# The middle tap of the last FFN's convolution made on ScalarE, with the weight cast of each half's last tile behind it

## The reference

```python
h = rms_norm_2(x, g_ffn[l])
up = depthwise_conv(h @ w_up[l], conv_f_w[l], conv_f_b[l], FFN_CONV // 2)
act = jax.nn.gelu(up[..., :D_FF_2], approximate=True) * up[..., D_FF_2:]
x = x + act @ w_down[l]
```

## Time and profile before

| what | us |
|---|---|
| median of three runs | 1883.85 |
| the profiled execution, its time | 1883.64 |
| the profiled execution, its span | 1881.9 |
| TensorE busy (matmuls) | 1855.5 |
| VectorE busy | 1243.5 |
| ScalarE busy | 523.6 |
| up phases of the last FFN, start of their first unit to end of their last | 1489 to 1626, 1695 to 1807 |

### The profile page before, as it was taken

One profiled execution on the slowest core, in us unless ns is written; L12 is line 12 of the kernel. 1 busy time (PEld: TensorE's weight loads), 2 busy tenths in 40 slices (PEclk: granted clock), 3 DMA queues, 4 the chain that ended last, 5 costly groups with the idle time before them and its releaser, 6 DMA issues.

```text
span 1881.9 us, 21566 instructions
## 1 busy us (share of the span) xinstructions
PE 1855.5 (99%) x8620; PEld 1482.7 (79%) x8620; DVE 1243.5 (66%) x1670; ACT 523.6 (28%) x481; POOL 15.4 (1%) x57
## 2 busy tenths in 40 slices
PE   8999999999999999999999999999999999999997
PEld 6888888878888778888888888877778888788875
DVE  6763667667745487443244779979975788726874
ACT  5333222122322222221122112148852122212210
POOL 0000000000000000000000000000000000000000
PEclk9999999999999999999999999999999999999998
DMA  5224341472111332222322224232224222232221
GB/s 203 89 82 153 111 157 64 149 263 99 68 68 46 112 134 76 103 84 84 122 90 72 84 90 157 90 112 85 76 70 162 90 90 98 75 104 103 81 72 71
DMA packets 48132, 194.64 MB, mean 103 GB/s; under 512 B 6720, under 2 KB 15296, under 8 KB 33344
## 3 DMA queue, kind: packets, MB, share of 16 engines
q1 hardware_dynamic: 48064, 193.70, 29.9%
HBM read 180.84 MB, written 12.85 MB: 103 GB/s over the span
## 4 chain that ended last, share of the span: by engine, by line
PE 77%; issue 20%; DVE 3%; DMA 0%; ACT 0%; POOLq 0%; POOL 0%; SPq 0%; DVEq 0%
PE bank L942 23%; PE bank L943 23%; PE bank L944 23%; PE xb L1217 2%; DVE wlo L1292 1%; PE xb L1163 0%; PE xb L1153 0%; PE bank L1059 0%; PE bank L1060 0%; PE bank L1061 0%; PE xb L1171 0%; PE xb L981 0%; PE xb L1120 0%; PE xb L974 0%; DVE x L1336 0%
## 5 line engine op out<-in xcount | busy, mean ns | idle before, releaser
L942 PE MATMUL bank<-uhi,whi 128*128 128x512 f32 x1552 | 622.9, 401 | 7.2 <-DVE wlo L2138 7.0
L943 PE MATMUL bank<-ulo,whi 128*128 128x512 f32 x1552 | 616.7, 397 | 0.0
L944 PE MATMUL bank<-uhi,wlo 128*128 128x512 f32 x1552 | 616.6, 397 | 0.0
L654 ACT ACTIVATE whi<-raw 128x2048 fp32r<-128x2048 f32 (+3 forms) x177 | 299.9, 1694 | 1101.8 <-PE bank L944 1073.1
L1292 DVE TENSOR_TENSOR wlo<-raw,whi 128x2048 fp32r<-128x2048 f32 (+3 forms) x177 | 356.5, 2014 | 80.3 <-ACT whi L654 77.9
L942 PEld LDWEIGHTS bank<-uhi,whi 128*128 128x128 f32 x1552 | 293.3, 189 | 80.2 <-issue 9.7
L944 PEld LDWEIGHTS bank<-uhi,wlo 128*128 128x128 f32 x1552 | 293.3, 189 | 71.6
L943 PEld LDWEIGHTS bank<-ulo,whi 128*128 128x128 f32 x1552 | 293.6, 189 | 71.0 <-issue 1.4
L942 PE MATMUL bank<-hhi,whi 128*128 128x512 f32 x528 | 209.8, 397 | 2.3 <-DVE hlo L1345 1.2
L943 PE MATMUL bank<-hlo,whi 128*128 128x512 f32 x528 | 209.3, 396 | 0.0
L944 PE MATMUL bank<-hhi,wlo 128*128 128x512 f32 x528 | 209.3, 396 | 0.0
(11 more groups left out here) (391 smaller groups left out, 1815.4 us busy)
## 6 DMA issues: line engine op xcount, KB each, us to landing
raw<-in_up SPq DMA_DIRECT2D x65, 1024.0 KB, 4.8
raw<-in_win SPq DMA_DIRECT2D x16, 1024.0 KB, 4.8
raw<-in_wout SPq DMA_DIRECT2D x8, 1024.0 KB, 4.9
raw<-in_down1a SPq DMA_DIRECT2D x8, 768.0 KB, 4.4
tab<-tab_kept SPq DMA_DIRECT2D x4, 1536.0 KB, 8.6
raw<-in_down2a SPq DMA_DIRECT2D x8, 768.0 KB, 4.4
raw<-in_down3a SPq DMA_DIRECT2D x8, 768.0 KB, 4.3
raw<-in_down1b SPq DMA_DIRECT2D x8, 640.0 KB, 4.0
```

Source lines behind the costliest of these rows:

```text
L654: act.activation(whi[s][:, 0:width], raw[s][:, 0:width], ACT.Copy).then_inc(w_hi, 1)
L942: pe.matmul(dst, wh, hi, start=first, stop=False)
L943: pe.matmul(dst, wh, lo, start=False, stop=False)
L944: return pe.matmul(dst, wl, hi, start=False, stop=last)
```

## The change

ScalarE makes the middle tap and the bias of both halves of each tile in the last FFN, as an `Identity` activation with the tap as its scale and the bias as its bias, both read from `vec`. It starts on the first half when VectorE's first scaling has been counted in the new semaphore `conv_half`, and on the second half at `evac[s]`, which VectorE already counted. The new semaphore `tapped` counts its two activations, and VectorE waits for each of them ahead of tap 0, where it made the middle tap itself before. On ScalarE the two activations stand between the weight cast and the gelu of each tile. In each half's last tile they stand ahead of the weight cast, so that the order there is taps, cast, gelu. The other two FFNs keep their code.

```diff
@@ semaphores
+        tapped = sem("tapped")
+        conv_half = sem("conv_half")
@@ block.scalar
-            def ffn(nb, func):
+            n_halves = Tally(conv_half)
+
+            def middle_taps(nb, turns, m):
+
+                s = nb % 2
+                for half, dst in ((0, cva), (1, cvb)):
+                    if half:
+                        act.wait_ge(evac[s], nb // 2 + turns)
+                    else:
+                        act.wait_ge(conv_half, n_halves.step())
+                    tap = vec[:, bass.ds(VECS["conv_f_w_2"] + 44 + 22 * half + m, 1)]
+                    bias = vec[:, bass.ds(VECS["conv_f_b_2"] + 22 * half + m, 1)]
+                    act.activation(dst[:, s, :], conv_src[:, half, :], ACT.Identity, scale=tap, bias=bias)\
+                        .then_inc(tapped, 1)
+
+            def ffn(nb, func, taps=False):
                 for h, tiles in enumerate(HALVES):
                     def up_turn(it):
                         alone = isinstance(it, int)
                         for j in range(2):
                             high(nb + j, it, UNIT)
                             if not (alone and it == 0):
+                                if taps:
+                                    middle_taps(nb + j, it, 2 * it + (j - 2 + sum(HALVES[:h])))
                                 gate_tile(nb + j, func)
 
                     def down_turn(it):
                         for j in range(2):
-                            high(nb + j, it, tiles * P)
+                            late = taps and j and isinstance(it, int) and it == 0
+                            if not late:
+                                high(nb + j, it, tiles * P)
                             if isinstance(it, int) and it == 0:
+                                if taps:
+                                    middle_taps(nb - tiles + j, tiles // 2, tiles - 2 + j + sum(HALVES[:h]))
+                                if late:
+                                    high(nb + j, it, tiles * P)
                                 gate_tile(nb - 2 + j, func)
 
                     up_turn(0)
-                    rolled_on(act, 1, tiles // 2, up_turn, [n_gates])
+                    rolled_on(act, 1, tiles // 2, up_turn, [n_gates, n_halves])
...
-            ffn(nb, ACT.Gelu_apprx_tanh)
+            ffn(nb, ACT.Gelu_apprx_tanh, taps=True)
@@ block.vector
+            taps_made = Tally(tapped)
@@ conv_tile
-                dve.tensor_tensor(out=conv_src[:, 0, :], in0=DB[s][0][:, :], in1=inv[:, :], op=ALU.mult)
+                dve.tensor_tensor(out=conv_src[:, 0, :], in0=DB[s][0][:, :], in1=inv[:, :], op=ALU.mult)\
+                   .then_inc(conv_half, 1)
...
-                    bias = vec[:, bass.ds(VECS["conv_f_b_2"] + 22 * half + m, 1)]
-                    then(dve.tensor_scalar(dst[:, s, :], src, tap[1], bias, ALU.mult, ALU.add))
+                    dve.wait_ge(tapped, taps_made.step())
                     then(dve.scalar_tensor_tensor(out=dst[:, s, 1:S], in0=src[:, 0:S - 1], scalar=tap[0],
                                                   in1=dst[:, s, 1:S], op0=ALU.mult, op1=ALU.add))
...
-                    rolled(dve, tiles // 2 - 1, up_turn, [gates, steps])
+                    rolled(dve, tiles // 2 - 1, up_turn, [gates, steps, taps_made])
```

## The result

The changed kernel takes 1881.11 us, the median of 22 runs (1880.02 to 1883.01), against 1884.24 us for the kernel before in the same job (22 runs, 1881.46 to 1885.89). The ratio is 0.9986, with a 95% interval of 0.9979 to 0.9992, a gain of 1.5 to 4.0 us. The forecast was 1882.0. The profiled execution took 1880.05 us, with a span of 1878.3 against 1881.9 us.

What follows compares the result with a forecast made beforehand. TensorE, busy 99% of the span, was taken as the bound, with gains only at its waits at the two turns. 0.92 + 0.97 = 1.9 us off 1883.85 gave 1882.0 us, range 1880.0 to 1884.8.

Steps and rivals of the forecast that it cites:

- The chain in the last tile: VectorE in each half's last tile: tap 0 0.34 us earlier, second middle tap's 0.58 gone, product 0.92 earlier.
- The turns: TensorE's waits where up phase becomes down phase: 0.92 us regained in the second half, 0.97 in the first.
- The looped tiles: 20 of 22 tiles run under a full TensorE: no gain, VectorE's wait grows from 0.28 to about 1.6 us.
- Table sets: Rival, chance 0.05: Identity and gelu share no table, two 1.28 us loads per tile, 1884.0 or 1886.8 us.
- The new wait: Rival, chance 0.12: late gelu in the last tiles or longer hand-overs between engines take the gain; 1882.9 us.
- The third rival: At the turn, low or a load rather than the convolution is last, so nothing moves: 1883.85 us, chance 0.03.
- the forecast's own 1881.8 to 1883.2: Whole-kernel time with a tap on ScalarE between 0.64 and 1.27 us, gaining 2.1 to 0.6 us, before noise.
- the wider range: Whole-kernel median of 1880.0 to 1884.8 us, allowing it to be off by 1 to 1.5 us either side.

Runs made afterwards that it cites:

- e1: Changed kernel, but ScalarE makes the middle taps only in each half's last tile, VectorE in the 20 others: 1881.82 us, 0.9991 of the kernel before.
- e2: Changed kernel, but ScalarE makes the middle taps only in the 20 other tiles, the last ones as before the change: 1883.84 us, 1.0002 of the kernel before.
- e4: Changed kernel with each middle tap made twice on ScalarE, first into a tile nobody reads: 1884.09 us, 1.0004 of the kernel before.
- e5: The changed kernel unaltered, run again beside the kernel before: 1881.54 us, ratio 0.9988.
- e8: The kernel of e1 unaltered, profiled once more: 1879.93 us in one timed run.
- e7: Kernel before, VectorE making all taps, with TensorE's waits and VectorE's low part split at the up-to-down turns: 1881.01 us, 0.9985 of the kernel before.

## Why the prediction was right

**Where the gain is.** The prediction put it wholly into the two last tiles. e1 and e2 cut the change along that line: 1.31 of the 1.67 us of losses go with the two last tiles alone, none with the other 20. The 0.36 us that e1 lacks are those of the late tap 0 in its own second half, which the changed kernel doesn't have; why is open.

**The chain in the last tile.** 0.92 us were forecast, 0.84 came. The second part, the 0.58 us of the second middle tap, was exact. The first was 0.26 instead of 0.34: VectorE took the first tap 0.10 us behind its end rather than 0.04, and the tap ended 0.02 us later. Tap durations (0.82 and 0.80 against 0.81 us) and their spacing (0.72 against 0.71) were right.

**The turns.** Forecast 0.92 + 0.97 = 1.9 us, measured 0.85 + 0.82 = 1.67. In the first half `wlo` came 0.04 us later than TensorE could have gone on, and so the longer interval behind a wait (0.10) stayed.

**The looped tiles.** 1.68 us of waiting was forecast as 1.6, nothing waits for `tapped`, and the taps' price in ScalarE's time could be doubled without notice (e4).

**The rivals.** Table sets: `Identity` shares the gelu's, for no load was added. By the Trainium skill, page "ScalarE: Activation LUTs", section "Table sets: the hidden batching unit", cheap functions are in every set, and the trace agrees, with 6 loads on the gelu's line before and after. The new wait: the hand-overs took 0.06 of the 0.08 us above, and the gelu was in time by 0.74 us rather than 0.44, and by 0.52 rather than 0.2 in the first half. Its operation came in at 0.61 us and began before the cast had ended, as ScalarE's operations overlap by some 0.1 us each. The third rival fell with the waits.

**What the forecast did not hold.** The mechanism was right, but the median was not 1882.0: it fell to 1881.11, below the forecast's own 1881.8 to 1883.2, against a kernel before whose median in that job was 0.4 us higher than the one reckoned from. Only the wider range, made for chance, holds it. The prediction also said that a change under 0.2% can't be told from none here; with 22 runs of each, the interval of 1.5 to 4.0 us excludes a change of nothing.

The spans of the two profiles differ by 3.6 us, of which the change made 1.67. VectorE's operation nearest to 47 us is 0.42 us earlier in the second profile, when nothing has been changed yet, and the rest, 1.5 us, lies at 1110 us, in the second mixer. The row of before, then that of after:

```profile
1110.00:1115.00 5.00, 5.00 (x17) 4.00 (x17) 1.78 (x10) 0.00 (x0) 1.64 (x1) 0.67 0.00 0
```

```profile
1110.00:1115.00 5.00, 5.00 (x22) 4.00 (x22) 1.73 (x10) 0.66 (x1) 1.64 (x1) 1.00 0.01 3
```

In both kernels TensorE waits 0.3 us there, runs 16 matmuls of one column in 1.95 us and goes back to the mixer's. In the profile of before the clock falls to half (1.2 GHz) 1.5 us later, at 1111.65, and its matmuls start 0.43 us apart until about 1115, when it rises again; in that of after they keep 0.234. That is 1.5 us, in code that the change doesn't touch. The profiles of e2, e5 and the second of e1 have no such dip there, the other five have. The kernel of e1 was profiled once with it (span 1880.6 us) and once without (1878.1). So it varies between executions of one kernel.

Whether it makes a part of the 2.2 and 3.1 us between medians can be asked of the timed runs, each of which has its mean granted clock on record, to three digits. No profile with the dip is above 0.996; without it the change, e5 and e8 have 0.997 and e2 has 0.996, for the mean also counts the tail, where the clock is at half in all. The changed kernel has 0.997 in 12 of its 22 runs and, in e5, in 5 of 11; the kernel before has it in 1 of 27 beside e5 and in 5 of 33 beside e1. Among the runs of e5's job at 0.996 the two kernels' medians are 1.4 us apart (6 and 16 runs) instead of 2.2. So what the medians show beyond 1.7 us goes, as far as these runs tell, with the clock and not with work saved. It is not a matter of taps: e7, without them, has 0.997 in 5 of 11 runs. Why some kernels get the higher mean more often is not shown.

## What to carry to other kernels

Under an engine that is busy for 99% of the time, price a change only where that engine waits; here 2 tiles of 22 held the whole gain, and the relief of VectorE by 20 x 1.38 = 28 us in the other 20 was worth nothing. At such a place the order in an almost idle engine's queue counts as much as the work: the same taps behind a cast of 1.3 or 1.5 us gave 0.5 us instead of 1.7. And before moving work to another engine, look at whether the consumer waits for more than it needs first: splitting the last hand-overs (e7) left 1.18 us of losses where moving the taps left 1.42, and both together left 0.34 of 3.1 us.

## What the runs showed of the hardware beside that

At half the granted clock the matmuls of 512 columns started 0.43 us apart, at the full one 0.234: a ratio of 1.82 and not 2. Each stop of TensorE cost 0.10 us on top of itself, as the interval behind it was 0.34 us; even behind the 0.04 us stop of the changed kernel's first half. The final norm's 8 matmuls of one column took 1.05 us in the profile of before, 1.41 in e2, 1.59 in e4 and 1.87 in e7; these differences of up to 0.8 us between spans lie in code common to all of them. They go with the moment at which the clock falls to half. In the profile of before the clock is full until 1869.4, behind the eight; in e2 and e4 it falls among them, at 1867.7 and 1868.3; in e7 it falls at 1866.6, ahead of them. The one-column matmuls start 0.11 us apart before the fall and 0.21 behind it. Before, then e7:

```profile
1868.11 1.05 PE L974 MATMUL xb<-ones,acc 128*128 128x1 f32 x8 [2.36 <-DVEq L1307]
```

```profile
1866.89 1.87 PE L989 MATMUL xb<-ones,acc 128*128 128x1 f32 x8 [2.36 <-DVEq L1324]
```

The start differs as well: the matmul that stands at 60.11 us in the profile of before stands at 59.2 to 60.8 in the ten profiles. Start, dip and tail together can move a span by more than the 1.67 us of the change.
